# Modulation weights multiplied in plain fp32 in four column groups, and streamed in another order in the lead

## The reference, cut to what matters

```python
sc, scc = silu(c), silu(c_ctx)                      # two vectors of 1024
for i in range(2):
    mod_lat = sc @ ada_w[i] + ada_b[i]              # ada_w[i]: 1024 x 6144
    mod_ctx = scc @ ada_w[i] + ada_b[i]
    sh1, sc1, g1, sh2, sc2, g2 = split(mod_lat, 6)  # and the same of mod_ctx
    a = rmsnorm(h, norm1_g[i]) * (1 + sc1) + sh1    # then mixer, gate, norm, FFN, gate
```

## Time and profile before

| | |
|---|---|
| median of three runs | 1642.07 us |
| the profiled execution | 1642.63 us, of which the span of the profile is 1641.1 |
| TensorE busy | 1495.9 us (91%) |
| VectorE, ScalarE, GpSimd busy | 1202.8, 766.6, 683.6 us |
| chain that ended last | TensorE 58%, VectorE 25%, issue 8%, ScalarE 4%, GpSimd 3% |
| `hi` (L685), `lo` (L1043 VectorE, L645 GpSimd) | 231 each: 441.2, 362.1 and 681.3 us |
| granted TensorE clock, mean | 0.963 |

### The profile page before, as it was taken

One profiled execution on the slowest core, in us unless ns is written; L12 is line 12 of the kernel. 1 busy time (PEld: TensorE's weight loads), 2 busy tenths in 40 slices (PEclk: granted clock), 3 DMA queues, 4 the chain that ended last, 5 costly groups with the idle time before them and its releaser, 6 DMA issues.

```text
span 1641.1 us, 28476 instructions
## 1 busy us (share of the span) xinstructions
PE 1495.9 (91%) x11030; PEld 1407.3 (86%) x11030; DVE 1202.8 (73%) x1665; ACT 766.6 (47%) x837; POOL 683.6 (42%) x240
## 2 busy tenths in 40 slices
PE   4999999979999996799999978799998999899997
PEld 4999988979998885699988867799997956799996
DVE  6544673675899998968999987976658775566656
ACT  5653564535333334554333345655455455455453
POOL 4775564445211124343111144456555500565552
PEclk9999999999999999899999997899999979999998
DMA  6675556345444445253544444455455500454551
GB/s 229 244 251 194 180 186 225 129 152 185 145 173 154 153 154 205 103 195 121 190 162 161 172 180 154 167 192 179 179 181 195 189 27 1 147 188 180 181 186 43
DMA packets 39029, 271.99 MB, mean 166 GB/s; under 512 B 4328, under 2 KB 5480, under 8 KB 6306
## 3 DMA queue, kind: packets, MB, share of 16 engines
q1 hardware_dynamic: 38946, 270.80, 46.0%
HBM read 269.72 MB, written 1.06 MB: 165 GB/s over the span
## 4 chain that ended last, share of the span: by engine, by line
PE 58%; DVE 25%; issue 8%; ACT 4%; POOL 3%; DVEq 2%; DMA 1%; POOLq 0%; ACTq 0%
PE ps L1555 16%; PE ps L1557 16%; PE ps L1556 16%; DVE sra L1161 8%; DVE wlo L1043 6%; POOL wlo L645 3%; PE ps L1609 2%; PE ps L546 2%; DVE rstd L1052 2%; ACT whi L685 2%; PE ps L1919 1%; DVE cva L466 1%; PE ps L1907 1%; DVE cvb L466 1%; DVEq L1161 1%
## 5 line engine op out<-in xcount | busy, mean ns | idle before, releaser
L645 POOL TENSOR_TENSOR wlo<-raw,whi 128x1024 fp32r<-128x1024 f32 (+2 forms) x231 | 681.3, 2953 | 930.5 <-ACT whi L685 930.4
L685 ACT ACTIVATE whi<-raw 128x2048 fp32r<-128x2048 f32 x231 | 441.2, 1912 | 612.9 <-PE ps L1557 449.5
L1043 DVE TENSOR_TENSOR wlo<-raw,whi 128x1024 fp32r<-128x1024 f32 (+2 forms) x231 | 362.1, 1571 | 309.9 <-ACT whi L685 309.6
L1555 PE MATMUL ps<-h_hi,whi 128*128 128x256 f32 x1656 | 478.6, 289 | 29.7 <-DVE h_lo L1092 11.6
L1556 PE MATMUL ps<-h_lo,whi 128*128 128x256 f32 x1656 | 472.8, 285 | 0.0
L1557 PE MATMUL ps<-h_hi,wlo 128*128 128x256 f32 x1656 | 472.5, 285 | 0.0
L1555 PEld LDWEIGHTS ps<-h_hi,whi 128*128 128x128 f32 x1656 | 322.0, 194 | 38.3 <-issue 21.3
L1556 PEld LDWEIGHTS ps<-h_lo,whi 128*128 128x128 f32 x1656 | 322.4, 195 | 0.2
L1557 PEld LDWEIGHTS ps<-h_hi,wlo 128*128 128x128 f32 x1656 | 322.1, 194 | 0.0
L1161 DVE SCALAR_TENSOR_TENSOR sra<-gates,cols,sra 128x256 f32<-128x256 f32 x480 | 240.9, 572 | 3.1 <-DVE sra L1161 2.9
L1555 PE MATMUL ps<-g_hi,whi 128*128 128x256 f32 x752 | 219.7, 292 | 20.5 <-issue 6.3
(11 more groups left out here) (242 smaller groups left out, 1973.4 us busy)
## 6 DMA issues: line engine op xcount, KB each, us to landing
raw<-w_dram SPq DMA_DIRECT2D x253, 1024.0 KB, 4.9
xlat<-xT_dram SPq DMA_DIRECT2D x1, 1024.0 KB, 4.8
brev<-bias_rows SPq DMA_DIRECT2D x1, 1024.0 KB, 9.1
brev<-ctxT_dram SPq DMA_DIRECT2D x1, 1024.0 KB, 6.8
out_dram<-xlat SPq DMA_DIRECT2D x4, 256.0 KB, 2.6
cols<-cols_dram SPq DMA_DIRECT2D x1, 512.0 KB, 5.7
gates<-tables_dram SPq DMA_DIRECT2D x1, 448.0 KB, 5.3
consts<-consts_dram SPq DMA_DIRECT2D x1, 192.0 KB, 10.1
```

The lines of the kernel that those rows point to most:

```text
L645: pool.tensor_tensor(wlo[:, g.slot, part], raw[:, g.slot, part], whi[:, g.slot, part].bitcast(F32), ALU.subtract).then_inc(lo2_done, 1)
L685: act.activation(whi[:, g.slot, :], raw[:, g.slot, :], ACT.Copy).then_inc(hi_done, 1)
L1043: dve.tensor_tensor(wlo[:, g.slot, part], raw[:, g.slot, part], whi[:, g.slot, part].bitcast(F32), ALU.subtract)\
L1555: pe.matmul(out, w[0], x[0], start=start, stop=False, skip_group_check=True)
```

## The change

All 48 modulation slabs are kept whole. `ada` multiplies `raw` in plain fp32: eight matmuls a slab, one for each k-tile, with a stationary operand of 32 columns; k-tile t goes to column group t mod 4, that is to the PSUM rows from 32 (t mod 4), so each group sums two k-tiles. `cnd` holds two plain fp32 columns for each k-tile, written by two Silu activations directly. `sel` has 128 rows and sums the four groups when the rows are turned; the copies out of PSUM have 128 rows.

In the lead the stream's order (`STREAM`) differs from TensorE's (`TURN`, the old `LEAD`): mix 0 comes ahead of ada 0 and ada 1, and from then on each modulation slab comes one place after the mix slab that TensorE multiplies behind it: mix 0, ada 0, ada 1, mix 1, ada 2, mix 2, ada 3, ... TensorE's order stays. `number()` gives the turn, for waits on the count of used slabs. At the start ScalarE and VectorE split slab 0 only.

```diff
+QUAD = 32
-AT = {item: n for n, item in enumerate(LEAD)}
+TURN = {item: n for n, item in enumerate(LEAD)}
+
+def lead_stream():
+    out = [LEAD[ADA_FIRST]] + LEAD[:ADA_FIRST]
+    rest = LEAD[ADA_FIRST + 1:]
+    while rest:
+        if rest[0][0] == "ada":
+            out += [rest[1], rest[0]]
+            rest = rest[2:]
+        else:
+            out.append(rest.pop(0))
+    return out
+
+STREAM = lead_stream()
+AT = {item: n for n, item in enumerate(STREAM)}
...
-ADA_WHOLE = set()
+ADA_WHOLE = {"lead", "ada_a", "ada_b", "ada_c", "ada_d", "ada_e"}
...
-            if use.startswith("ada"):
+            if use == "lead":
+                out.append(STREAM[i][0] == "ada" and use in ADA_WHOLE)
+            elif use.startswith("ada"):
...
     def number(self):
+        if not self.n and self.c < len(STREAM):
+            return TURN[STREAM[self.c]]
         return self.c + 3 * self.n * self.j
...
-        cnd = sb("cnd", [P, 4 * MOST * KT + P], F32R)
-        cnd_at = 4 * (MOST - 1)
-        cnd4 = cnd[:, cnd_at:cnd_at + 4 * MOST * KT].rearrange("p (k f) -> p k f", f=4 * MOST)
+        cnd = sb("cnd", [P, 2 * (MOST - 1) + QUAD * KT])
+        cnd_at = 2 * (MOST - 1)
+        cnd2 = cnd[:, cnd_at:cnd_at + QUAD * KT].rearrange("p (k f) -> p k f", f=QUAD)
-        sel = sb("sel", [4 * MOST, 2 * MOST])
+        sel = sb("sel", [P, 2 * MOST])
-        modrow = cvb[0:4 * MOST, 1, :, :]
-        late_rows = cvb[0:4 * MOST, 0, 0, :]
+        modrow = cvb[:, 1, :, :]
+        late_rows = cvb[:, 0, 0, :]
...
-            act.activation(tiny[:, 0:16], cols[:, COL["cond"][0]:COL["cond"][0] + 2 * KT], ACT.Silu).then_inc(cond_f, 1)
-            act.wait_ge(cond_f, 1)
             act.wait_ge(cond_zero, 1)
             for s in range(2):
-                act.activation(cnd4[:, :, 2 * s], tiny[:, 8 * s:8 * s + 8], ACT.Copy).then_inc(cond_hi, 1)
+                c = COL["cond"][0] + KT * s
+                act.activation(cnd2[:, :, s], cols[:, c:c + KT], ACT.Silu).then_inc(cond_f, 1)
+            hi(Slab(0))
             root(0)
-            hi(Slab(0))
-            hi(Slab(1))
             split_hi(0, bufA, h_hi)
-            hi(Slab(2))
...
-            dve.wait_ge(cond_hi, 2)
-            for s in range(2):
-                dve.tensor_tensor(cnd4[:, :, 2 * s + 1], ..., ALU.subtract).then_inc(cond_lo, 1)
-            scale_split(0, xlat, ..., first=lambda: lo(Slab(0)), second=lambda: lo(Slab(1)))
-            lo(Slab(2))
+            scale_split(0, xlat, ..., first=lambda: lo(Slab(0)))
...
             def ada(g, bank, k=0, n=1):
-                w = weights(g, KT)
+                pe.wait_ge(landed[g.slot], g.landings())
+                w = raw[:, g.slot, :].rearrange("p (k n) -> p k n", k=KT)
                 for t in range(KT):
-                    for part in range(2):
-                        c = cnd_at + 4 * MOST * t - 4 * k
-                        ins = pe.matmul(ps[:, bank, 0:SLABC], cnd[:, c:c + P], w[part][:, t, :],
-                                        start=(t == 0 and part == 0 and k == 0), stop=(t == KT - 1 and part == 1 and k == n - 1),
-                                        skip_group_check=True)
+                    r, c = QUAD * (t % 4), cnd_at + QUAD * t - 2 * k
+                    ins = pe.matmul(ps[r:r + QUAD, bank, 0:SLABC], cnd[:, c:c + QUAD], w[:, t, :], start=(t < 4 and k == 0),
+                                    stop=(t >= 4 and k == n - 1), skip_group_check=True)
                 ins.then_inc(slab_done, 1)
...
-                    ada(Slab(n), ada_bank(g), g % MOST, MOST)
+                    ada(Slab(AT[kind, g]), ada_bank(g), g % MOST, MOST)
...
-    sel = np.kron(np.eye(2 * MOST, dtype=np.float32), np.ones((2, 1), np.float32))
+    sel = np.zeros((P, 2 * MOST), np.float32)
+    for r in range(0, P, QUAD):
+        sel[r:r + 2 * MOST] = np.eye(2 * MOST)
```

More of the change, by code:

```diff
@@ L337, in build @@
         tap0, conv_out, silu_done, mid_f, mid_hi, mid_lo = sem("tap0_done"), sem("conv_done"), sem("silu_done"), sem("mid_done"), sem("mid_hi_done"), sem("mid_lo_done")
-        cond_f, cond_zero, cond_hi, cond_lo = sem("cond_done"), sem("cond_cleared"), sem("cond_hi_done"), sem("cond_lo_done")
+        cond_f, cond_zero = sem("cond_done"), sem("cond_cleared")
         row_done, modT_done, mod_done, amod_done = sem("mod_rows_done"), sem("mod_turned"), sem("mod_done"), sem("amod_done")
@@ L721, in mod_rows @@
                     act.wait_ge(modT_done, q - 1)
-                act.activation(modrow[:, q % 2, :], ps[0:4 * MOST, ada_bank(i), 0:SLABC], ACT.Copy).then_inc(row_done, 1)
+                act.activation(modrow[:, q % 2, :], ps[:, ada_bank(i), 0:SLABC], ACT.Copy).then_inc(row_done, 1)
             def hi_ahead(use, k0, k1):
@@ L731, in group_rows @@
                 slabs = group_slabs(use)
-                n = len(slabs)
                 act.wait_ge(slab_done, slabs[-1] + 1)
-                act.activation(late_rows[0:4 * n, :], ps[0:4 * n, GROUP_BANKS[use][0], 0:SLABC], ACT.Copy).then_inc(rows_done, 1)
+                act.activation(late_rows, ps[:, GROUP_BANKS[use][0], 0:SLABC], ACT.Copy).then_inc(rows_done, 1)
             def glu(q, j, g):
@@ L871, in _ @@
             hi(Slab(b0 + 2 + RING))
-            act.wait_ge(slab_done, AT["mix", N_MIX - 1] + 1)
+            act.wait_ge(slab_done, TURN["mix", N_MIX - 1] + 1)
             split_hi(1, ctx_y, h_hi, shift_of(0, 0, 1))
@@ L1241, in _ @@
             H, G = (h_hi, h_lo), (g_hi, g_lo)
-            dve.memset(cnd[:, :].bitcast(F32), 0.0).then_inc(cond_zero, 1)
+            dve.memset(cnd[:, :], 0.0).then_inc(cond_zero, 1)
             dve.memset(relb[BUCKETS:BUCKETS + 1, :], NEG).then_inc(s_relb, 1)
             fold(0, bufB)
-            dve.wait_ge(cond_hi, 2)
-            for s in range(2):
-                dve.tensor_tensor(cnd4[:, :, 2 * s + 1], tiny[:, 8 * s:8 * s + 8], cnd4[:, :, 2 * s].bitcast(F32), ALU.subtract)\
-                   .then_inc(cond_lo, 1)
-            scale_split(0, xlat, lambda t: col("norm_mix", t), 0, bufA, H, None, first=lambda: lo(Slab(0)), second=lambda: lo(Slab(1)))
-            lo(Slab(2))
+            scale_split(0, xlat, lambda t: col("norm_mix", t), 0, bufA, H, None, first=lambda: lo(Slab(0)))
             dve.wait_ge(tab_done, 1)
@@ L1618, in turn_rows @@
                     c = T + 2 * n * m
-                    ins = pe.matmul(ps[:, bank, c:c + 2 * n], rows[0:4 * n, m * P:m * P + P], sel[0:4 * n, 0:2 * n],
+                    ins = pe.matmul(ps[:, bank, c:c + 2 * n], rows[:, m * P:m * P + P], sel[:, 0:2 * n],
                                     start=(m == 0), stop=True, skip_group_check=True)
@@ L1633, in _ @@
             means(0)
-            pe.wait_ge(cond_lo, 2)
+            pe.wait_ge(cond_f, 2)
             for n, (kind, g) in enumerate(LEAD):
@@ L1647, in _ @@
                     if 5 <= g < 9 or 13 <= g < 15:
-                        tokens(Slab(n), n % 4, H)
+                        tokens(Slab(AT[kind, g]), n % 4, H)
                     else:
-                        features(Slab(n), n % 4, H, tiles=1 if g == 0 else 2, split=0 if g == 0 else None)
+                        features(Slab(AT[kind, g]), n % 4, H, tiles=1 if g == 0 else 2, split=0 if g == 0 else None)
                 if n == 0:
```

## The result

The changed kernel took 1579.21 us in the median of four runs (1576.28 to 1582.18), the kernel before 1641.59 beside it: a ratio of 0.9613, 95% interval 0.9585 to 0.9641. The forecast was 1586 us, between 1570 and 1611. The profiled execution has a span of 1578.3 us, 62.8 less than before; the sum of the forecast was 56.7.

A forecast was written before the change was run, and what follows sets the result against it. TensorE bounds the lead, VectorE's layer-norm chain with splits inside it the FFN tails. Gains 33 (lead) + 10 + 10 + 2.7 + 1 = 56.7 us, from 1642.6 to 1586; 8-in-10 range 1570 to 1611.

The forecast's parts named there:

- A slab on TensorE: Lone modulation slab: four column groups run side by side, 0.054 us a record, 1.2 us instead of 1.89.
- the rivals' prices for it, 3.6 and 2.0: Modulation slab: groups not side by side, 3.6 us, 1655 in all (5%); only two at a time, 2.0, 1608 (12%).
- The start: Up to mix 1: mix 0 streamed and split first, so mix 1 starts at 28.6 instead of 40.1; 10 us gained.
- The rest of the lead: From mix 1 to the lead's end: cheaper modulation slabs and no split waits; whole lead 261.5 instead of 294.6.
- The condition: Lead: loads and splits of mix g+2 and the next modulation slab are ready over 3 us before they are due.
- Groups a and b: Tails of ffn0 and ffn_ctx: earlier down slab and splits gone from VectorE's chain, less 1 for clock; 10 us each.
- Group c: Ahead of ffn_lat: two VectorE splits go, but ffn_lat's first load and ScalarE's root behind it limit the gain; 2.7 us.
- Groups d and e: Later modulation groups, same effects without the long wait ahead: d about +1.5, e about -0.5; together -3 to +5 us.
- Held `raw` slots: Rival, lead: whole slabs holding load slots make loads land late and pace it, 1 us on 21 pairs; 1607 us, 15%.

The follow-up runs named there:

- e1: Changed kernel with all eight k-tiles of a modulation slab in one 32-column group, 32 rows copied and summed; 1649.66 us.
- e2: Changed kernel with k-tile t in column group t mod 2, so two groups side by side, 64 rows copied and summed; 1605.47 us.
- e4: Changed kernel with the second layer's 24 modulation slabs split again, both parts multiplied in plain fp32 in four groups; 1601.35 us.
- e7: Changed kernel with last modulation-row copy and ada_c's root ahead of splits, and three modulation slabs ahead of ffn2's norm sum; 1577.90 us.
- e3: Changed kernel with the lead's loads streamed in TensorE's order again (ada 0, ada 1, mix 0, ada 2, mix 1, ...); 1618.68 us.
- e5: Changed kernel with one modulation slab ahead of the last down slab and five behind (three and three before), tails of ffn0 and ffn_ctx; 1577.12 us.

## Why the prediction was right, step by step

*A slab on TensorE.* 1.2 forecast, 1.19 measured, because the rows of two groups were carried on to four; e1 and e2 show the rivals' prices for it, 3.6 and 2.0, as 3.76 and 2.04, worked out like the 1.19. The sum stood up as well: the rivals' times of 1655 and 1608 were 69 and 22 us above the forecast, and e1 and e2 took 70.5 and 26.3 more than the changed kernel.

*The start*, 10 forecast, 8.5 found. Mix 1 started at 29.9 instead of 28.6, and took 7.47 us at a granted clock of 0.77, 1.7 more than before, where 1.5 was put. The step that was wrong is "gets its `whi` behind `h_hi` to 25.1": mix 0 and mix 1 are numbers 0 and 3 of the new stream and share a slot of `whi`, so that ScalarE waited for TensorE's last matmul of mix 0:

```profile
24.40 1.91 ACT L708 ACTIVATE whi<-raw 128x2048 fp32r<-128x2048 f32 x1 [2.27 <-PE ps L1571]
```

*The rest of the lead*, 23 forecast, 27.2 found. The condition held: from mix 2 on the splits of every mix slab were done 2.8 to 13.9 us before TensorE began it, and no pair waited. A modulation slab between two mix slabs saves 0.70 us, as put (1.89 - 1.2), 14.7 for 21 of them. The 4.2 us that the sum lacked are elsewhere. The new idle time is 4.4 us where 4 was put, but the old one was worth more than its 12.5, because a lower clock stood behind it: after the wait of 4.1 in the earlier trace rows mix 21 itself took 7.29 us at a granted clock of 0.80, so that with the wait it took 11.34 us where it takes 5.94 now. And a modulation slab behind attention matmuls saves up to 1.10 instead of 0.70, some 1.6 us in all. Both are plain fp32, so a saved change of form would fit, but no run isolates it.

*Groups a and b*, 10 each forecast, 11.9 and 10.3 found. The closeness of b is partly luck, since between executions of the same stretch it would be 7 to 10, and in a the sum came out for partly wrong reasons. The landing was 0.7 us sooner than put (590.5, 7.6 behind the last slab of ffn0, where 8.3 was assumed). The clock was sized wrong: "if all of the 3.77 ... doubled only half of that, 1.9, would be lost" is no bound. The idle time put nearly all 16 records at 1.2 GHz (granted clock 0.54), so they took 6.76, 3.0 us lost where I took 1; in group b they took 5.40 (0.68). The pieces of the chain that went are right: 5.3 us from centring to reciprocal, where 5.5 was forecast (2.92 + 3.55, less about 1 for the squares). What made up for the clock was not in the sum: VectorE's multiplication without GpSimd beside it (3.94 to 2.36, 1.6 us), and the end of the group, where TensorE stood idle for 5.66 us in front of pw1_lat before and 1.45 now, and the slab behind took 7.6 us before and 6.0 now. e4 gives the same picture from the other side: with the splits back 8.0 and 8.3 us of the 11.9 and 10.3 return. The rest, 3.9 and 2.0, is of the size by which these stretches differ between executions of the same code (3.4 and 3.3), and no cause of it is shown.

*Group c*, 2.7 forecast, 3.0 found: ffn_lat's first slab landed at 975.9 and got its `whi`, and the root stood behind it, as put:

```profile
975.95 1.91 ACT L708 ACTIVATE whi<-raw 128x2048 fp32r<-128x2048 f32 x1 [5.55 <-DMA raw<-w_dram]
977.77 0.46 ACT L724 ACTIVATE rstd<-ps,epsc 128x256 f32<-128x256 f32 x1
```

e7 took the root out of that place and won 1.3 us. The prediction had that load go out when TensorE has used the second modulation slab, so TensorE's price sets its time, and e2 bears this out: with no splits but slabs of 2.04 us c gains 0.7 us (29.6 to 28.9) instead of 3.0.

*Groups d and e*, +1 forecast, 0.0 found, inside their bounds. The 1.8 us in pw1_lat and ffn_ctx weren't forecast; most of them can be the difference between executions, and no run here isolates a cause.

*The rivals.* Held `raw` slots were the right thing to fear (15%): they don't pace the lead in the order of the change, but in the order before they cost 40 us (e3). The prediction timed the loads in the new order only, and so never said that the whole gain in the lead rests on it.

## What to carry to other kernels

Price a small stationary operand by its column groups: plain fp32 with two vectors costs 3.57 us a slab in one group and 1.00 in four, and it frees three engines of a split. An operand that is multiplied straight from the load buffer holds that buffer until the matmul; give its place in the stream to the operands with a longer preparation, or the gain turns into waits and lower clock (here 40 us). When a wait is moved away from the end of a stage, look first at what the freed engine will then run beside: at the end of the lead VectorE's own split took 3.27 us instead of 1.23 once the wait was gone. And before a gain of 2 or 3 us in one stretch is believed, look at the same stretch in profiles of other kernels that don't touch it: here tail b differed by 3.3 us by itself.

## What was not expected of the hardware

Records of four column groups start within 0.02 us of each other and a new set every 0.22 us, the spacing of single records in one group. A TensorE that waited 4.7 us in two pieces for loads (3.3 and 1.4, with a modulation slab between) had its next 16 records of plain fp32 in 6.76 us instead of 3.65 (e5), where I had expected a third of that loss. Of VectorE's and GpSimd's two-operand instructions the second to start seems to wait for the first: a VectorE subtraction of 1.23 us took 3.27, and one of 128 columns up to 4.06, when GpSimd's had begun 0.23 and 0.33 us before. The small splits in the earlier trace rows fit that too: GpSimd's parts, begun first and 4.26 us long, were done at 641.0 and 650.9, and VectorE's at 641.2 and 651.0.
